# TensorE's wait for the low halves of the weights: one wait for two units in place of one for each

## The chip, the cores and the metric

The kernel runs on one core of one Trainium2 chip. The metric is the device time of one execution in microseconds (us), lower is better. A run's time is the median of several executions of the same program on the chip, and a profile is the record that the hardware profiler made of one execution.

## The reference

The input is a sequence of 256 tokens of width 2048 in float32. Two transformer blocks follow each other.

```
# block 1
h = x + fox_mixer(rms_norm(x))          # 16 heads of 128, causal softmax with a forget gate
h = h + conv_ffn(rms_norm(h))           # up to 2 x 5632, 3-tap convolution, silu(gate) * val, down
# block 2
a = rms_norm(h); qa, ka, va, ra, ga, qb, kb, vb = split(a @ w_in)
log_g = log_sigmoid(ga @ gate_w2 + gate_b) / 16
out_a = gla_mixer(qa, ka, va, ra, log_g)        # 4 heads, chunks of 64, gated linear attention
out_b = dilated_mixer(rms(qb), rms(kb), vb, rel_bias)   # 8 heads, three dilation patterns
h = h + concat(out_a, out_b) @ w_out
h = h + (silu(n @ w_gate) * (n @ w_up)) @ w_down, with n = rms_norm(h)
```

The time goes to the products with the weights: in all 788 x 0.5 MiB of float32 weights pass through the core once.

## The kernel before, in words

The weights are stored as one stream of 788 units. A unit is a tile of 128 partitions x 1024 float32 values, that is eight blocks of 128 x 128. Activations lie transposed (features on partitions, 256 tokens along the free axis), and each product is made from split numbers: a weight is written as a high half `whi` and a low half `wlo`, both in the format float32r, and the activations likewise as `x[:, kc, 0, :]` and `x[:, kc, 1, :]`. For each block TensorE multiplies `whi` with both halves of the activations (512 columns) and `wlo` with the high half (256 columns). VectorE later folds the two 256-column halves of the PSUM bank into one (L943).

Four slots (RING = 4) hold units in flight, each with `raw`, `whi` and `wlo`. Unit u lies in slot u mod 4. A unit passes through these steps:

- SyncE loads it into `raw[slot]` (L278), once the low half of the unit four before it is made.
- ScalarE copies `raw` to `whi` (split_hi, L654). It waits for the load, and for `unit_used`, which says that TensorE is done with the unit four before it.
- VectorE makes `wlo = raw - whi` (split_lo, L937) and raises `lo_ready` by one.
- TensorE waits for `lo_ready` and runs the 16 matmuls of the unit (L345 and L346). The last one raises `unit_used`.

The order of each engine's work is written out by hand. With AHEAD = 3, step k of ScalarE's and VectorE's programs splits unit k + 3, among the other work of that step: VectorE takes finished chunks out of PSUM (take, L943 and L977, which raises `chunk_out`), does the softmax, the gates and the residual sums, and ScalarE does squares, exponentials, logarithms and copies. TensorE's own order is units in sequence, with small matmuls between them.

The stages in order are: one unit pair for the forget gates (units 0 and 1), the heads of layer 1 with six units each (from unit 2), its output projection, up projection (from unit 130) and down projection (from unit 306), then the same for layer 2 (from unit 394): one unit pair for the gate ranks, four gated heads of 12 units from unit 396, eight heads of six units, output, up and down projection. Most stages are hardware loops in which the unit's number is a register's value. Every loop advances by a multiple of four units, so a unit's slot is known when the program is built and an even slot is an even unit.

At the start, VectorE does in this order: low halves of x chunks 0 to 3, split of unit 0, x chunks 4 to 11, split of unit 1, x chunks 12 to 15, splits of units 2 and 3, eight sums of squares (L970), split of unit 4, eight more sums, split of unit 5, split of unit 6, the forget gates' take and first steps (L943 to L1187), the first head's query take, split of unit 7. ScalarE makes the high halves in the same order, with the squares between the splits of 3 and 4 and of 4 and 5. Behind the high half of unit 5 it waits for the mean of squares, which TensorE makes behind unit 4 (norm_mean, L366), for rstd by a Ln (L667) and an Exp (L669), and only then makes the high halves of 6 and 7. TensorE's unit 6 waits for the forget gates' take as well (`chunk_out`). Behind unit 7 stands the first head's mean (head_mean, L371), which waits for ScalarE's squares of query and key (L674).

In the first gated head TensorE makes the gates' matmuls (L598) behind unit 398. VectorE and ScalarE turn them into decays (L1304 to L1317, L904 to L911) ahead of the splits of units 402 and 403. Behind unit 403 stand the matmuls of L428, which wait for `g_kd` (L1096).

Of the kernel before, what the change touches and what calls it, by code (L numbers as in the profile page):

```python
# [96 lines left out]
def build(nc, wstream, xt, vectors, identity, dist_onehot, rel_bias, gate_w2, scan_keep, gla_mask, fox_mask, out):  # L97
    with ExitStack() as ctx:
# [3 lines left out]
        def sem(name):  # L102
            return ctx.enter_context(nc.semaphore(name))
# [108 lines left out]
        hi_ready, lo_ready, unit_used = sem("hi_ready"), sem("lo_ready"), sem("unit_used")  # L212
# [122 lines left out]
        def _(pe):  # L335
            def unit(pos, k, blocks, x):

                slot = pos.slot(k)
                pe.wait_ge(lo_ready, pos.unit(k) + 1)
                for j, (bank_no, kc, first, last, late) in enumerate(blocks):  # L340
                    if late:
                        pe.wait_ge(*late)
                    w_hi = whi[slot][:, j * P:(j + 1) * P]
                    w_lo = wlo[slot][:, j * P:(j + 1) * P]
                    pe.matmul(acc[bank_no][:, :], w_hi, x[:, kc, :, :].rearrange("p a s -> p (a s)"), start=first, stop=False)  # L345
                    mm = pe.matmul(acc[bank_no][:, S:2 * S], w_lo, x[:, kc, 0, :], start=False, stop=last)  # L346
                mm.then_inc(unit_used, 1)

            def half(pos, k, bank_no, part, x, late=None):

                late = late or {}
                unit(pos, k, [(bank_no, 8 * part + j, part == 0 and j == 0, part == 1 and j == 7, late.get(8 * part + j))
                              for j in range(BLOCKS)], x)
# [180 lines left out]
            def down(layer):  # L534

                with pe.Fori(0, 2) as i:
                    pos = Pos(layer.unit_down, U_DOWN // 2, i)

                    pe.wait_ge(hid_split, FC * (layer.n + 1) - 1)
                    for k in range(U_DOWN // 2):  # L540
                        blocks = []
                        for b in range(BLOCKS * k, BLOCKS * (k + 1)):
                            c, kc = divmod(b, FC)
                            if kc == 0:
                                pe.wait_ge(chunk_out, layer.chunk_down + 8 * i + c - 3)

                            late = (hid_split, FC * (layer.n + 1)) if b == FC - 1 else None
                            blocks.append((c % 4, kc, kc == 0, kc == FC - 1, late))
                        unit(pos, k, blocks, hid2)
# [52 lines left out]
            for c in range(6):  # L602
                pe.wait_ge(chunk_out, L1.chunk_heads + c - 2)
                for part in range(2):
                    k = 2 * c + part
# [12 lines left out]
            for j in range(2):  # L618
                chunk = DIL.chunk0 + 3 * j
                n = DIL.count0 + j  # L620
                for c in range(3):
                    pe.wait_ge(chunk_out, chunk + c - 2)
                    for part in range(2):
                        k = 2 * c + part
# [823 lines left out]
```

## Time and profile before

| | us |
|---|---|
| median of 3 runs (2330.54 to 2330.74) | 2330.71 |
| the profiled execution | 2330.62 |
| its span, first to last instruction | 2328.8 |
| TensorE matmuls busy | 2306.4 (99%) |
| VectorE busy | 1611.0 (69%) |
| ScalarE busy | 1220.8 (52%) |

Busy times count instructions that work on data. TensorE's matmuls and weight loads are shown as two engines, PE and PEld, since they overlap; both are issued by one sequencer. DVE is VectorE, ACT is ScalarE, SP is SyncE. Starts are counted from the beginning of the span. "L345" is line 345 of the kernel.

### The profile page before, as it was taken

Reading aid. Unit: us, or ns where it says so; the run is one execution under the profiler, and the core shown is the slowest. Engines: PE = TensorE matmul, PEld = TensorE weight load, DVE = VectorE, ACT = ScalarE, POOL = GpSimd, SP = SyncE. Lnnn points to the kernel's source line nnn. Section 1 sums busy time; section 2 is a strip of 40 time slices with the busy share of each in tenths; the row PEclk is TensorE's granted clock in tenths of the full one; section 3 lists DMA queues with packets and bytes.
Section 4 is the critical chain, followed back from the end, with each engine's and each line's share of the span. In section 5 each row is a group of like instructions: output and inputs, shape, how many; then the busy total and the mean of one; then the engine's idle time right before and its main releaser. Section 6 shows DMA issues by size and latency. Waiting matters only on the chain.

```text
span 2328.8 us, 39072 instructions
## 1 busy us (share of the span) xinstructions
PE 2306.4 (99%) x13218; PEld 1998.6 (86%) x13218; DVE 1611.0 (69%) x2339; ACT 1220.8 (52%) x1574; POOL 22.3 (1%) x45
## 2 busy tenths in 40 slices
PE   7999999999999999999999999999999999999999
PEld 5888888888888888888878888888888888888888
DVE  7767677788888888555566667677666667664554
ACT  6666665655555555444455466655444444443332
POOL 0000000000000000000000000000000000000000
PEclk9999999999999999999999999999999999999999
DMA  6555545555555555655555444455555555555553
GB/s 213 166 168 179 176 161 182 186 191 189 186 191 191 189 186 184 198 189 186 188 165 165 166 159 160 158 184 189 189 189 189 189 189 190 189 188 192 198 193 131
DMA packets 118513, 423.39 MB, mean 182 GB/s; under 512 B 13629, under 2 KB 15829, under 8 KB 118464
## 3 DMA queue, kind: packets, MB, share of 16 engines
q1 hardware_dynamic: 114048, 415.29, 53.6%
q0 software_dynamic: 1968, 5.13, 0.8%
q10 hardware_dynamic: 2448, 2.32, 0.3%
q8 instruction: 31, 0.51, 0.1%
q14 instruction: 18, 0.15, 0.0%
HBM read 420.55 MB, written 3.70 MB: 182 GB/s over the span
## 4 chain that ended last, share of the span: by engine, by line
PE 97%; DVE 1%; ACT 0%; issue 0%; DMA 0%; SPq 0%; DVEq 0%; ACTq 0%
PE acc L345 62%; PE acc L346 31%; PE b_mean L371 1%; PE b_score L382 0%; DMA xres<-xt 0%; DVE wlo L937 0%; PE b_turn L390 0%; PE b_mean L463 0%; PE b_mean L464 0%; PE b_score L381 0%; PE b_mean L396 0%; PE b_val L377 0%; PE b_mean L397 0%; PE b_mean L398 0%; DVE sq_sum L970 0%
## 5 line engine op out<-in xcount | busy, mean ns | idle before, releaser
L345 PE MATMUL acc<-xs,whi 128*128 128x512 f32 x4384 | 1549.2, 398 | 15.3 <-DVE wlo L937 12.9
L654 ACT ACTIVATE whi<-raw 128x1024 fp32r<-128x1024 f32 x788 | 831.5, 1059 | 871.6 <-PE acc L346 862.4
L937 DVE TENSOR_TENSOR wlo<-raw,whi 128x1024 fp32r<-128x1024 f32 x788 | 961.4, 1223 | 407.2 <-ACT whi L654 403.9
L346 PE MATMUL acc<-xs,wlo 128*128 128x256 f32 x4384 | 1225.8, 280 | 0.0
L345 PEld LDWEIGHTS acc<-xs,whi 128*128 128x128 f32 x4384 | 823.1, 188 | 213.4 <-DVE wlo L937 14.9
L346 PEld LDWEIGHTS acc<-xs,wlo 128*128 128x128 f32 x4384 | 828.3, 189 | 5.5 <-issue 5.3
L345 PE MATMUL acc<-hid,whi 128*128 128x512 f32 x1408 | 494.5, 395 | 0.0
L346 PE MATMUL acc<-hid,wlo 128*128 128x256 f32 x1408 | 396.4, 282 | 0.0
L943 DVE TENSOR_REDUCE folded_t<-acc 128x256 f32<-128x512 f32 (+1 forms) x338 | 233.3, 690 | 158.4 <-PE acc L346 146.9
L345 PEld LDWEIGHTS acc<-hid,whi 128*128 128x128 f32 x1408 | 264.8, 188 | 62.2
L346 PEld LDWEIGHTS acc<-hid,wlo 128*128 128x128 f32 x1408 | 264.4, 188 | 0.0
L345 PE MATMUL acc<-mix,whi 128*128 128x512 f32 x512 | 182.6, 398 | 0.0
L346 PE MATMUL acc<-mix,wlo 128*128 128x256 f32 x512 | 144.5, 282 | 0.0
L345 PEld LDWEIGHTS acc<-mix,whi 128*128 128x128 f32 x512 | 96.2, 188 | 23.5 <-issue 0.5
L346 PEld LDWEIGHTS acc<-mix,wlo 128*128 128x128 f32 x512 | 96.3, 188 | 0.5 <-issue 0.5
L769 ACT ACTIVATE hid<-hid 128x256 f32 (+1 forms) x88 | 36.0, 409 | 52.4 <-DVE hid L1140 52.2
L984 DVE SCALAR_TENSOR_TENSOR qk_n<-qk,qk_gain,rstd_qk 128x256 f32<-128x256 f32 x48 | 21.1, 482 | 53.1 <-ACT rstd_qk L680 53.1
L977 DVE TENSOR_TENSOR up_v<-folded_t,rstd 128x256 f32<-128x256 f32 x88 | 37.5, 427 | 3.0
L977 DVE TENSOR_TENSOR up_g<-folded_t,rstd 128x256 f32<-128x256 f32 x88 | 37.5, 426 | 3.0
L1144 DVE TENSOR_TENSOR hid<-hid,hid 128x256 f32 (+1 forms) x88 | 36.9, 419 | 1.0 <-ACT hid L769 1.0
L754 ACT ACTIVATE tap_g<-up_g,vec 128x256 f32<-128x256 f32 x44 | 26.5, 602 | 16.3 <-DVE up_g L977 16.3
L762 ACT ACTIVATE tap_v<-up_v,vec 128x256 f32<-128x256 f32 x44 | 26.5, 603 | 15.3 <-DVE up_v L977 15.2
(169 smaller groups left out, 924.9 us busy)
## 6 DMA issues: line engine op xcount, KB each, us to landing
raw<-wstream SPq DMA_DIRECT2D x788, 512.0 KB, 3.4
xres<-xt SPq DMA_DIRECT2D x4, 512.0 KB, 8.3
decay_row<-decay_scratch POOLq DMA_DIRECT2D x16, 128.0 KB, 3.5
out<-xres ACTq DMA_DIRECT2D x16, 128.0 KB, 2.3
dist_scratch<-bias_scratch POOLq DMA_DIRECT2D x8, 192.0 KB, 3.7
toeplitz<-dist_scratch POOLq DMA_DIRECT2D x8, 128.0 KB, 3.8
vec<-vectors ACTq DMA_DIRECT2D x1, 213.5 KB, 5.2
g_keep<-scan_keep POOLq DMA_DIRECT2D x1, 128.0 KB, 3.1
```

The lines of the kernel that those rows point to most:

```text
L345: pe.matmul(acc[bank_no][:, :], w_hi, x[:, kc, :, :].rearrange("p a s -> p (a s)"), start=first, stop=False)
L346: mm = pe.matmul(acc[bank_no][:, S:2 * S], w_lo, x[:, kc, 0, :], start=False, stop=last)
L371: pe.matmul(b_mean[:, :], mean_h[:, :], sq_qk[:, :, :].rearrange("p a s -> p (a s)"), start=True, stop=True).then_inc(qk_mean, 1)
L654: act.activation(whi[slot][:, :], raw[slot][:, :], ACT.Copy).then_inc(hi_ready, 1)
L754: act.activation(tap_g[:, :], up_g[:, 0:S], ACT.Identity, scale=column("conv0", j), bias=column("convb", j)).then_inc(tap0, 1)
L762: act.activation(tap_v[:, :], up_v[:, 0:S], ACT.Identity, scale=column("conv0", FC + j), bias=column("convb", FC + j)).then_inc(tap0, 1)
L769: act.activation(hid2[:, j, 0, :], hid[:, :], ACT.Copy).then_inc(hid_hi_ready, 1)
L937: dve.tensor_tensor(wlo[slot][:, :], raw[slot][:, :], whi[slot][:, :], ALU.subtract).then_inc(lo_ready, 1)
L943: dve.tensor_reduce(folded_t[0:rows, :], acc[bank_no][0:rows, :].rearrange("p (a s) -> p s a", a=2), AX_X, ALU.add).then_inc(chunk_folded, 1)
L977: dve.tensor_tensor(dst, folded_t[0:rows, :], rstd[0:rows, :], ALU.mult).then_inc(chunk_out, 1)
L984: dve.scalar_tensor_tensor(out=qk_n[:, a, :], in0=qk[:, a, :], scalar=qk_gain[:, col + a:col + a + 1], in1=rstd_qk[:, a, :], op0=ALU.mult, ...
L1144: dve.tensor_tensor(hid2[:, j, 1, :], hid[:, :], hid2[:, j, 0, :], ALU.subtract).then_inc(hid_split, 1)
```

## The change

Only units in even slots wait for `lo_ready`, and they wait for one unit more: their own low half and that of the unit behind them. Units in odd slots have no wait of their own.

```diff
             def unit(pos, k, blocks, x):
 
                 slot = pos.slot(k)
-                pe.wait_ge(lo_ready, pos.unit(k) + 1)
+                if slot % 2 == 0:
+                    pe.wait_ge(lo_ready, pos.unit(k) + 2)
                 for j, (bank_no, kc, first, last, late) in enumerate(blocks):
```

## Rows read from the trace of the kernel before

**Rows 1.** The page, part 1: busy us (share of the span) xinstructions.

```profile
PE 2306.4 (99%) x13218; PEld 1998.6 (86%) x13218; DVE 1611.0 (69%) x2339; ACT 1220.8 (52%) x1574; POOL 22.3 (1%) x45
```

**Rows 2.** View of waits, PEld: engine, line, released by: us in total, times, longest.

```profile
PEld acc L345 <- DVE wlo L937: 14.9, 6, 11.0
```

**Rows 3.** Page, part 5: count | busy, mean ns | idle before.

```profile
L937 DVE TENSOR_TENSOR wlo<-raw,whi 128x1024 fp32r<-128x1024 f32 x788 | 961.4, 1223 | 407.2 <-ACT whi L654 403.9
```

**Rows 4.** Timeline of PEld, 11 to 45 us: start, us, what [idle before <-releaser].

```profile
11.04 0.29 PEld L345 LDWEIGHTS acc<-xs,whi 128*128 128x128 f32 x1 [11.04 <-DVE wlo L937]
...
15.88 0.19 PEld L345 LDWEIGHTS acc<-xs,whi 128*128 128x128 f32 x1 [0.29 <-DVE wlo L937]
...
18.69 0.19 PEld L345 LDWEIGHTS acc<-xs,whi 128*128 128x128 f32 x1
...
25.24 0.19 PEld L345 LDWEIGHTS acc<-xs,whi 128*128 128x128 f32 x1 [0.95 <-DVE wlo L937]
...
29.29 0.30 PEld L366 LDWEIGHTS b_mean<-sq_sum,mean_d 128*128 128x128 f32 x2 [1.32 <-DVE sq_sum L970]
...
30.88 0.19 PEld L345 LDWEIGHTS acc<-xs,whi 128*128 128x128 f32 x1 [0.87 <-DVE wlo L937]
...
36.38 0.19 PEld L345 LDWEIGHTS acc<-xs,whi 128*128 128x128 f32 x1 [2.73 <-DVE f L977]
...
39.60 0.19 PEld L345 LDWEIGHTS acc<-xs,whi 128*128 128x128 f32 x1 [0.49 <-DVE wlo L937]
...
44.06 0.30 PEld L371 LDWEIGHTS b_mean<-sq_qk,mean_h 128*128 128x128 f32 x2 [1.69 <-issue]
```

**Rows 5.** View of line 339 (the wait): register operations, ns min/median/max, starts.

```profile
L339 PEldq ALU_OP  x651: 32/32/42, 63.4 to 2319.3; - x163
```

**Rows 6.** Timeline at unit 308, of PEld and of DVE.

```profile
928.32 0.19 PEld L345 LDWEIGHTS acc<-hid,whi 128*128 128x128 f32 x1
...
927.32 3.69 DVE L937 TENSOR_TENSOR wlo<-raw,whi 128x1024 fp32r<-128x1024 f32 x3
```

**Rows 7.** Timeline of DVE at the start: the splits of units 1, 5 and 7.

```profile
14.60 1.23 DVE L937 TENSOR_TENSOR wlo<-raw,whi 128x1024 fp32r<-128x1024 f32 x1 [0.44 <-ACT whi L654]
...
29.60 1.23 DVE L937 TENSOR_TENSOR wlo<-raw,whi 128x1024 fp32r<-128x1024 f32 x1 [0.37 <-ACT whi L654]
...
38.33 1.22 DVE L937 TENSOR_TENSOR wlo<-raw,whi 128x1024 fp32r<-128x1024 f32 x1
```

**Rows 8.** Timeline of ACT at the start: table load, Ln, square of the key.

```profile
29.59 1.28 ACT L667 ACT_TABLE_LOAD   x1
30.88 0.47 ACT L667 ACTIVATE ln_x<-b_mean,eps 128x256 f32<-128x256 f32 x1
...
43.53 0.42 ACT L674 ACTIVATE sq_qk<-qk 128x256 f32<-128x256 f32 x1 [1.79 <-DVE qk L977]
```

**Rows 9.** Timeline at units 402 and 403, of PEld and of DVE.

```profile
1193.35 0.19 PEld L345 LDWEIGHTS acc<-xs,whi 128*128 128x128 f32 x1
...
1197.35 0.19 PEld L345 LDWEIGHTS acc<-xs,whi 128*128 128x128 f32 x1 [1.22 <-DVE wlo L937]
...
1201.82 0.31 PEld L428 LDWEIGHTS b_score<-g_qt,g_kt 128*64 128x64 f32 x8 [1.69 <-DVE g_kd L1096]
...
1196.08 2.35 DVE L937 TENSOR_TENSOR wlo<-raw,whi 128x1024 fp32r<-128x1024 f32 x2
```

**Rows 10.** Timeline at unit 424, of PEld and of DVE (split of 425).

```profile
1270.94 0.19 PEld L345 LDWEIGHTS acc<-xs,whi 128*128 128x128 f32 x1
...
1269.24 1.22 DVE L937 TENSOR_TENSOR wlo<-raw,whi 128x1024 fp32r<-128x1024 f32 x1
```

**Rows 11.** Timeline of PE; and the windows view (PEclk is the granted clock).

```profile
11.84 0.63 PE L345 MATMUL acc<-xs,whi 128*128 128x512 f32 x1
...
2325.18 0.28 PE L346 MATMUL acc<-hid,wlo 128*128 128x256 f32 x1
...
2329.30:2330.00 0.70, 0.00 (x0) 0.00 (x0) 0.00 (x0) 0.00 (x0) 0.00 (x0) 0.50 0.00 0
```

## Prediction

> **What bounds the kernel now.** I read the page's busy shares first: TensorE works 99% of the span [rows 1]. So any idle time added to TensorE comes out at the end one for one, unless it fills idle time that is there already. Next comes the view of waits, taken on TensorE's weight loads because the wait that is changed stands ahead of them: waits for VectorE's `wlo` (the low halves) sum to only 14.9 us in 6 places, 11.0 of it ahead of the first unit [rows 2]. Then the group of L937: the split itself takes 1.22 us a unit [rows 3]. A unit of TensorE takes 2.81 us (15.88 to 18.69 [rows 4]), so a split normally has room. What matters is how early the low half of unit u+1 lies before unit u starts. I numbered the units by their first weight load and matched them with the 788 splits, in order. The program's own order fixes this lead: at step k ScalarE and VectorE split unit k+3, after unit k-1 has freed its slot. So while unit u runs, the split of u+3 is made, and at the start of u those of u+1 and u+2 are normally there.
>
> **What the change removes.** Odd units (every second one, 394 of 788) lose their wait. TensorE's sequencer shows 651 register operations of 32 ns at that line over the run, as far as the waits stand in loops [rows 5]. They run beside matmuls: the loads of unit 1 to unit 2 and unit 308's show no extra pitch [rows 4, 6]. I book 0. The bounds: nothing, and a gain of half of them, 325 x 0.032 = 10.4 us, if each were exposed. The first is far nearer to the rows, since a whole 8-block unit at 2.81 us holds no stall at its edge.
>
> **What it adds.** An even unit u now waits for the split of u+1 too. No split is made later for that reason alone, until TensorE itself is late. Behind TensorE's wait stand all its later matmuls, and behind those `unit_used` (ScalarE's next splits, VectorE's takes) and the next weight load. The wait bites in three places.
>
> (1) The start, units 0 to 8. Unit 1's split ends at 14.60 + 1.23 = 15.83 [rows 7]; unit 0 starts there, at 15.88, and no longer at 11.04. Units 0 to 3 then run back to back: 4.55 us for the first (11.04 to 15.88 less 0.29 idle [rows 4], it is slow) and 3 x 2.81, to 28.9. Unit 2 needs the splits of 2 and 3. These use their slots for the first time, so nothing of TensorE holds them, and before the two units ran without a pause (18.69 to 25.24 less 0.95 idle is 2 x 2.8 [rows 4]): the split of 3 is made by 21.5, and unit 2 now starts at 23.2, no wait. Unit 4 (25.24 before) must wait for the split of unit 5, 29.60 + 1.23 = 30.83 [rows 7]. That one does not move: ScalarE's share of it stands behind its squares, and unit 1, whose slot it needs, is done at 23.2. So all that was lost in units 0 to 3 is hidden behind this later wait. Unit 4 starts at 30.88 and ends at 33.7.
> Behind unit 4 stands the sum-of-squares matmul (norm_mean), 29.29 before [rows 4], at 33.7 now. Its result was early before: ScalarE's Ln waited for its table until 29.59 + 1.28 = 30.87 and started at 30.88 [rows 8]. Now the mean lands at 33.7 + 0.7 = 34.4, Ln starts near 34.5: 3.6 us late. From there to the split of unit 7 VectorE and ScalarE hold no slack (Ln, table, Exp, split 6, forget-gate take, query take, split 7), so it ends at 38.33 + 1.22 + 3.6 = 43.15 [rows 7]. TensorE meanwhile does norm_mean and the distance bias (their weight loads ended 0.87 us ahead of 30.88, at 30.0; with the bias matmuls some 1.2 us from 29.29, an estimate) and unit 5, 35.0 to 37.8. Unit 6 before waited only for the forget-gate take, to 36.38, and unit 7 for its own split, to 39.60 [rows 4]. Now unit 6 waits for the split of unit 7 and starts at 43.2; unit 7 follows without a pause and ends at 43.2 + 2 x 2.82 = 48.85. The head's mean matmul (L371), which waited for ScalarE's square until 44.06 before [rows 4, 8], finds it done (43.95 + 3.6 = 47.6) and goes at 48.85. So the start costs 48.85 - 44.06 = 4.8 us. Unit 8 then asks for the split of 9, made near 48.2: no wait.
>
> (2) Unit 308, third of the first down projection. The convolution's last work holds up VectorE; three splits run together from 927.32 for 3.69 us, the first of which is unit 309's, done at 928.54, against a start of unit 308 at 928.32 [rows 6]. Cost 0.27 us.
>
> (3) Unit 402, where layer 2's gates are made. The gate chain holds the split of unit 403 to 1196.08 + 1.22 = 1197.30. Before, unit 402 ran from 1193.35 under it, and TensorE waited 1.22 us ahead of 403 and 1.69 ahead of the L428 matmuls for `g_kd` [rows 9]. Now unit 402 starts at 1197.36, 403 at 1200.18, and L428 at 1203.0 in place of 1201.82: `g_kd` depends on neither unit, so of the 4.0 us of stall 2.8 fill idle time that was there. Cost 1.2 us.
>
> Elsewhere the u+1 split is early enough. The smallest margin in the repeated stages is that of the second gated head: unit 425's split ends at 1269.24 + 1.22 = 1270.46, unit 424 starts at 1270.94 [rows 10], 0.48 us left (three such heads); the same subtraction for the even units of the other repeated stages gives 1.1 us or more. These margins move with TensorE, so the delays above do not eat them.
>
> Sum: 4.8 + 0.27 + 1.2 = 6.2 us, no gain against it.
>
> (4) The clock. The first matmul of unit 0 shown takes 0.63 us [rows 11], and the unit 4.55 in place of 2.81: 1.2 GHz at first, 2.4 GHz soon after. TensorE's longest idle before was 2.73 us on the weight loads (36.38 [rows 4]), and unit 6 behind it ran at full pace. After the last matmul, which ended at 2325.18 + 0.28 = 2325.46 [rows 11], the granted clock was down to 0.50 by 2329.30, 3.8 us later. The new stall ahead of unit 6 is 37.8 to 43.2, over 5 us. So here I expect the clock to fall, and units 6 and 7 to pay for it in full, as nothing behind them waits for anyone else. Price: that of the cold first unit, 4.55 - 2.81 = 1.7 us; bounds 0 (it holds) and twice that, 3.5 (it comes back late). The stall ahead of 402, 3.8 us, stands on the edge; I leave it warm in the sum.
> The Trainium skill (TensorE: Matmul & The Clock Gate, section "Why this matters for your kernels") says the same of idle gaps between bursts: one long enough throws the clock back to half, and it calls the moment variable from run to run. By that rule both stalls may pay; by the 2.73 us row alone neither would. No run yet decides for gaps between.
>
> Total: 6.2 + 1.7 = 7.9 us. The profiled execution took 2330.62 (span 2328.8 and 1.8 around it), the median is 2330.71; 2330.7 + 7.9 = 2338.6.
>
> **Rivals.**
> A. The clock holds over both stalls: 2330.7 + 6.2 = 2336.9. For it: no gap before ever cost pace. Against: 0.50 at 3.8 us after the last matmul.
> B. The clock falls at both stalls, or comes back late: 6.2 + 2 x 1.7 = 9.6, so 2340.3; with the late return at the first, 2342.
> C. The start's loss is mostly hidden: units 6 and 7 overlap a wait that I took as moving (say the Ln chain shortens because its table is already loaded, or the take of unit 7 has slack). Then 2 to 4 us are left in all: 2333 to 2335, within 0.2%. Against it: the split of unit 7 at 38.33 has no idle time ahead of it [rows 7], so VectorE came to it straight from its chain.
> D. The other side: dropped waits give pace. If TensorE's sequencer, not its array, sets the time at odd units, each of the register operations saved is worth its 32 ns: 10.4 us off, 6.2 on, 2326.5 with a warm clock. It decides in favour from 19 ns saved per odd unit (7.9/394 = 0.020 us). Against: no idle mark stands at unit 2's start, whose wait had long been met [rows 4].
> E. The new condition bites in every repeated head, as semaphores arrive later than the profile's ends: 0.48 us of margin would have to be lost, three times; under 1 us, inside the range.
>
> **How the numbers follow.** Forecast (falls once) 0.44, A 0.30, B 0.13, C 0.08, D 0.05. A change under 0.2% (4.7 us, 2326.0 to 2335.4) can't be told from none. The range takes in the forecast with its own bounds, A less 1.1 us for the estimates in its chain (the 3.6, the 1.2), and B's lower price with 0.9 above it: 2335.8 to 2341.2. Slower by over 0.2% has the forecast, A and B, 0.87; within holds C and part of D, 0.10; faster 0.03.
>
> **What would show it.** Right: the first weight load of unit 0 at 15.9, unit 4's at 30.9, unit 6's near 43.2 with over 5 us idle ahead put down to `wlo` L937; L371 near 50.5 (48.9 if the clock held); hi matmuls of unit 6 at 0.63; a stall near 4 us ahead of unit 402 while that ahead of L428 is gone; unit 308 with 0.27. The waits for `wlo` grow from 14.9 us to about 31 (15.9 + 2.0 + 5.3 + 0.3 + 4.0 and some), yet the end moves by under 10, as part of that fills old waits. Wrong: stalls on `wlo` in the repeated stages; L371 before 47 us; pace changes in the steady stages; a total under 2335.4.

## The result, and the profile after

| | before | after |
|---|---|---|
| median, us | 2330.58 (2330.47 to 2330.74, 5 runs) | 2341.80 (2340.47 to 2344.92, 5 runs) |
| ratio | 1 | 1.0053 (95%: 1.0041 to 1.0064) |
| profiled execution, us (its span) | 2330.62 (2328.8) | 2341.80 (2340.0) |
| TensorE matmuls busy, us | 2306.4 | 2311.1 |

The change costs 11.2 us, where 7.9 was forecast. All line numbers of the changed kernel are one higher from line 340 on (TensorE's high matmul is L346 there, the split L938, L371 is L372).

The weight loads of the changed kernel at the start. They answer to [rows 4].

```profile
15.80 0.29 PEld L346 LDWEIGHTS acc<-xs,whi 128*128 128x128 f32 x1 [15.80 <-DVE wlo L938]
...
20.88 0.33 PEld L346 LDWEIGHTS acc<-xs,whi 128*128 128x128 f32 x1
...
24.17 0.19 PEld L346 LDWEIGHTS acc<-xs,whi 128*128 128x128 f32 x1
...
30.82 0.19 PEld L346 LDWEIGHTS acc<-xs,whi 128*128 128x128 f32 x1 [1.15 <-DVE wlo L938]
...
33.64 0.30 PEld L367 LDWEIGHTS b_mean<-sq_sum,mean_d 128*128 128x128 f32 x2
...
35.01 0.19 PEld L346 LDWEIGHTS acc<-xs,whi 128*128 128x128 f32 x1 [0.64 <-issue]
...
43.16 0.29 PEld L346 LDWEIGHTS acc<-xs,whi 128*128 128x128 f32 x1 [5.38 <-issue]
...
48.24 0.33 PEld L346 LDWEIGHTS acc<-xs,whi 128*128 128x128 f32 x1
...
51.50 0.30 PEld L372 LDWEIGHTS b_mean<-sq_qk,mean_h 128*128 128x128 f32 x2
...
52.04 0.19 PEld L346 LDWEIGHTS acc<-xs,whi 128*128 128x128 f32 x1 [0.24 <-issue]
```

The starts on which the chain rests are where it put them: unit 0 at 15.80, unit 4 at 30.82, the mean of squares at 33.64, unit 5 at 35.01, unit 6 at 43.16. Between them unit 2 came at 24.17 and not at 23.2: units 0 and 1 together took 8.4 us (15.80 to 24.17), where the chain had 7.4. Unit 4's wait shrank by it (1.15 us idle), so it cost nothing. From unit 6 on the two part. Units 6 and 7 take 8.3 us to L372 (43.16 to 51.50) and not 5.7. The 5.38 us stall of the weight loads carries the mark "issue", but the view of the matmuls names the split for it, and for the stall ahead of unit 402:

```profile
43.19 0.77 PE L346 MATMUL acc<-xs,whi 128*128 128x512 f32 x1 [5.09 <-DVE wlo L938]
...
1207.97 0.77 PE L346 MATMUL acc<-xs,whi 128*128 128x512 f32 x1 [3.81 <-DVE wlo L938]
```

The next two fences show ScalarE and VectorE on the chain that made the split of unit 7 late, and answer to [rows 8] and [rows 7].

```profile
29.52 1.28 ACT L668 ACT_TABLE_LOAD   x1
34.38 0.47 ACT L668 ACTIVATE ln_x<-b_mean,eps 128x256 f32<-128x256 f32 x1 [3.57 <-PE b_mean L367]
```

```profile
41.83 1.22 DVE L938 TENSOR_TENSOR wlo<-raw,whi 128x1024 fp32r<-128x1024 f32 x1
```

The Ln starts 3.5 us later than before, now on TensorE's mean. The split of unit 7 ends at 43.05, and unit 6 starts 0.1 us after it.

One matmul of unit 6, and the windows view over both places (busy time of each engine, then the granted clock, DMA share and GB/s):

```profile
43.97 0.63 PE L346 MATMUL acc<-xs,whi 128*128 128x512 f32 x1
```

```profile
39.00:42.00 3.00, 0.00 (x0) 0.00 (x0) 2.86 (x8) 1.10 (x2) 0.00 (x0) 1.00 0.53 175
42.50:49.20 6.70, 6.01 (x19) 5.18 (x20) 5.56 (x10) 3.58 (x7) 1.06 (x2) 0.50 0.51 169
49.30:52.00 2.70, 2.70 (x15) 2.20 (x15) 1.41 (x2) 0.51 (x1) 0.17 (x1) 1.00 0.76 206
1202.00:1206.00 4.00, 2.16 (x13) 1.60 (x11) 3.96 (x6) 3.42 (x4) 0.00 (x0) 1.00 0.25 101
1206.50:1213.20 6.70, 5.23 (x16) 4.49 (x17) 5.71 (x9) 2.13 (x3) 0.00 (x0) 0.50 0.58 168
```

The clock fell to 0.50 (1.2 GHz) while TensorE still stood, at either stall, and stayed there for most of two units each time. (The view prints 1.00 ahead of the trace's first record of the clock too, so the slow start has to be read from the weight loads: 0.33 us at 20.88, 0.19 at 24.17.) Around unit 402 the weight loads, which answer to [rows 9]:

```profile
1207.94 0.29 PEld L346 LDWEIGHTS acc<-xs,whi 128*128 128x128 f32 x1 [4.11 <-issue]
1213.02 0.29 PEld L346 LDWEIGHTS acc<-xs,whi 128*128 128x128 f32 x1
...
1216.14 0.31 PEld L429 LDWEIGHTS b_score<-g_qt,g_kt 128*64 128x64 f32 x8 [0.25 <-issue]
```

The 1.69 us wait for `g_kd` is gone, as forecast, but unit 402 takes 5.08 us and 403 3.1.

At unit 308, TensorE's weight loads for the high halves and VectorE's splits, which answer to [rows 6]:

```profile
935.90 0.19 PEld L346 LDWEIGHTS acc<-hid,whi 128*128 128x128 f32 x1 [0.32 <-DVE wlo L938]
...
938.00 0.19 PEld L346 LDWEIGHTS acc<-hid,whi 128*128 128x128 f32 x1
938.37 0.19 PEld L346 LDWEIGHTS acc<-hid,whi 128*128 128x128 f32 x1
938.71 0.19 PEld L346 LDWEIGHTS acc<-hid,whi 128*128 128x128 f32 x1
```

```profile
934.63 3.69 DVE L938 TENSOR_TENSOR wlo<-raw,whi 128x1024 fp32r<-128x1024 f32 x3
```

The stall is the forecast 0.27 us (a pitch of 0.62 in place of 0.35). But behind it the pitch of a block is no longer 349 ns throughout: it runs 349, 351, 360 in turn, 353.3 in the mean, for the 86 units that are left of the stage. Counting TensorE's matmuls in 30 us (first and second down projection), before:

```profile
1000.00:1030.00 30.00, 30.00 (x174) 26.28 (x174) 16.74 (x19) 13.08 (x15) 0.00 (x0) 1.00 0.58 188
2200.00:2230.00 30.00, 30.00 (x172) 26.16 (x171) 15.17 (x15) 11.16 (x11) 0.00 (x0) 1.00 0.56 191
```

and after:

```profile
1000.00:1030.00 30.00, 30.00 (x173) 26.13 (x172) 16.72 (x19) 12.71 (x15) 0.00 (x0) 1.00 0.55 186
2200.00:2230.00 30.00, 30.00 (x174) 26.27 (x173) 15.42 (x15) 11.64 (x11) 0.00 (x0) 1.00 0.63 199
```

The counts alone are coarse; the starts of units 310 to 393 and 704 to 787 give 348.9 and 353.3 ns a block before, 353.3 and 348.9 after, at full clock in each.

Comparing the starts of the same unit in the two profiles gives the whole account: +7.45 us at unit 8, settling at +7.31 by unit 20; +0.27 at unit 308; +3.05 over the rest of the first down projection; +3.69 at unit 404; -3.09 over the second down projection. Sum 11.2, the difference of the spans.

### The profile page after: what moved, and what is told of

The parts are those of the page before. It is cut to its first block, busy times and chain, and to the rows that moved or that the text cites. A ratio compares the mean times of both kernels' runs of the same rounds, so it can differ in the third digit from the quotient of the medians.

```text
span 2340.0 us, 38704 instructions
## 1 busy us (share of the span) xinstructions
PE 2311.1 (99%) x13218; PEld 1998.6 (85%) x13218; DVE 1610.9 (69%) x2339; ACT 1220.8 (52%) x1574; POOL 22.3 (1%) x45
## 4 chain that ended last, share of the span: by engine, by line
PE 98%; DVE 1%; DMA 0%; ACT 0%; issue 0%; SPq 0%; DVEq 0%; ACTq 0%
PE acc L346 62%; PE acc L347 31%; PE b_mean L372 1%; PE b_score L383 0%; DMA xres<-xt 0%; PE b_turn L391 0%; DVE wlo L938 0%; PE b_mean L464 0%; PE b_mean L465 0%; PE b_score L382 0%; PE b_mean L397 0%; PE b_val L378 0%; PE b_mean L399 0%; PE b_mean L398 0%; DVE sq_sum L971 0%
## 5 line engine op out<-in xcount | busy, mean ns | idle before, releaser
L346 PE MATMUL acc<-xs,whi 128*128 128x512 f32 x4384 | 1554.2, 400 | 25.5 <-DVE wlo L938 25.5
L938 DVE TENSOR_TENSOR wlo<-raw,whi 128x1024 fp32r<-128x1024 f32 x788 | 961.2, 1223 | 414.5 <-ACT whi L655 411.3
L346 PEld LDWEIGHTS acc<-xs,whi 128*128 128x128 f32 x4384 | 826.4, 189 | 228.2 <-issue 18.6
L346 PE MATMUL acc<-hid,whi 128*128 128x512 f32 x1408 | 494.5, 395 | 0.0
L346 PEld LDWEIGHTS acc<-hid,whi 128*128 128x128 f32 x1408 | 264.7, 188 | 62.8 <-DVE wlo L938 0.3
L346 PE MATMUL acc<-mix,whi 128*128 128x512 f32 x512 | 182.6, 398 | 0.0
L346 PEld LDWEIGHTS acc<-mix,whi 128*128 128x128 f32 x512 | 96.2, 188 | 23.7 <-issue 0.5
```

Source lines behind the costliest of these rows:

```text
L938: dve.tensor_tensor(wlo[slot][:, :], raw[slot][:, :], whi[slot][:, :], ALU.subtract).then_inc(lo_ready, 1)
```

## The experiments

Theory after the result: the waits cost what was forecast (6.3), half clock behind both long stalls costs some 2.5 each, and the paces of the down projections cancel in this pair of profiles. Rivals: a loss spread over the steady stages; late splits and not the clock behind the stalls; a pace drawn by chance and untouched by the change.

**Undoing the places one by one.** In the changed kernel, the units of the named places wait for themselves again:

```diff
-                if slot % 2 == 0:
+                u = pos.base + k
+                if not pos.per and (u < 8):        # e1;  e2: 402 <= u < 404;  e3: both
+                    pe.wait_ge(lo_ready, u + 1)
+                elif slot % 2 == 0:
                     pe.wait_ge(lo_ready, pos.unit(k) + 2)
```

`pos.base` is the number of a stage's first unit, and `pos.per` is 0 outside loops. e4 is e3 with `pos.base == 306 and k in (2, 3)` added: units 308 and 309, and 352 and 353, which have their places in the loop's second pass.

> Units 0 to 7 wait as in the kernel before; all other units wait in pairs. Theory (stalls plus clock): the start costs the change 4.8 us of waiting and 2.5 us of half clock (unit 8 starts 7.4 us later in the profile after), so this comes back 7.3 us below the changed kernel, near 2334.5, with unit 8 at 44.6 and no clock fall before unit 402; the stall and the fall at 402 stay. Rival (the loss is spread over the steady stages, as the waits or the pace of the matmuls got worse everywhere): under 3 us come back.

> Only units 402 and 403 wait as before; all others wait in pairs. Theory: 1.2 us of waiting and 2.5 us of half clock come back at 402, so 3.7 us below the changed kernel, near 2338.1; the low clock is granted once, behind the start. Rival: the clock falls there because of the long gate stage itself, not because of the stall: then only 1.2 us come back and the profile shows a low clock there still.

> Units 0 to 7 and 402 and 403 wait as before, all others in pairs. Theory: only the 0.27 us stall ahead of unit 308 is left, no clock fall: 2331.0, but the pace of the two down projections may differ from before by 3.1 to 3.3 us each (353 ns a block in place of 349, or the other way round), as it did in the profile after. If the stall at 308 sets the slow pace of the first down projection, that stage is slow here and fast in the fourth kernel. Rival: odd waits dropped make the steady stages faster or slower by a part of a nanosecond a block, seen in the starts of units 130 to 306.

> Units 0 to 7, 402 and 403 wait as before, and so do the units in the places of 308 and 309 in the down projections' loop of layer 1; all others in pairs. Theory: no stall is left: 2330.7 if the pace of the down projections is that of the kernel before. If the stall at 308 is what turned the first down projection from 349 to 353 ns a block, it is at 349 here. If it is not the stall but where the stage's instructions lie, or chance, it need not be.

| kernel | median, us | range | runs | ratio to before (95%) |
|---|---|---|---|---|
| e1, start undone | 2334.99 | 2333.50 to 2338.06 | 10 | 1.0025 (1.0016 to 1.0035) |
| e2, 402 undone | 2338.25 | 2337.00 to 2338.50 | 6 | 1.0038 (1.0026 to 1.0051) |
| e3, both undone | 2330.83 | 2330.53 to 2333.90 | 10 | 1.0004 (0.9994 to 1.0014) |
| e4, and 308 | 2330.68 | 2327.48 to 2333.83 | 10 | 0.9999 (0.9988 to 1.0010) |
| before, beside them | 2330.50 | 2327.39 to 2334.10 | 27 | |

Against the changed kernel's 2341.8, 6.8 and 3.6 us come back, where 7.3 and 3.7 were expected, and nothing measurable is left when both places are undone. The medians mix the levels told of below, so the starts of units are the firmer ground: e1 starts unit 8 at 44.89, 7.15 us sooner than the changed kernel, and e2 takes 3.80 us less than it from unit 394 to unit 404 (33.91 and 37.71). Units 140 to 300 take 443.73 us (346.7 ns a block) in every profile of this document, with the odd waits or without them, so some 390 dropped waits are worth nothing either way: the spread loss and the gain from fewer waits both fall. In e2 the clock stayed at 1.00 through the gate stage; its stalls there are those of before (1.22 and 1.69 us), so the long gate stage alone does not bring the clock down.

In e1's profile one thing was not expected, though the start is that of the kernel before:

```profile
36.53 0.24 PEld L350 LDWEIGHTS acc<-xs,whi 128*128 128x128 f32 x1 [2.73 <-DVE f L982]
...
40.86 0.19 PEld L350 LDWEIGHTS acc<-xs,whi 128*128 128x128 f32 x1
...
44.89 0.19 PEld L350 LDWEIGHTS acc<-xs,whi 128*128 128x128 f32 x1 [0.39 <-issue]
```

```profile
36.70:40.00 3.30, 3.30 (x11) 2.82 (x12) 3.23 (x9) 2.44 (x5) 0.00 (x0) 0.50 0.48 159
```

Here the same 2.73 us wait as in [rows 4] did bring the clock down, and unit 6 took 4.33 us. Unit 8 still started only 0.3 us later than before: the wait for the split and for the square behind it swallowed the loss. So my argument from that row, that a gap of 2.73 us costs no pace, rested on one execution.

**The three levels.** The executions of the kernel before, which lay within 0.3 us at first, fell into three groups in the later comparisons: near 2327.5, 2330.6 and 2333.8. They are 3.1 us apart, as a down projection at 353.3 and one at 348.9 are (704 blocks x 4.4 ns), and the profiles agree: both stages are fast in e6's of 2327.54, one is slow in e3's and e4's of 2330.7 and 2330.8, both are in e5's of 2333.96. In the four sets of runs beside the experiments their numbers were 13/8/6, 7/17/3, 15/11/3 and 3/2/4. e3, which keeps the stall at 308, had none of 10 in the lowest group; e4, without it, had 4 of 10. Hence the next two, each one edit of the kernel before, which asks for more at one even unit and drops no wait:

```diff
-                pe.wait_ge(lo_ready, pos.unit(k) + 1)
+                pe.wait_ge(lo_ready, pos.unit(k) + (2 if pos.base == 306 and k == 2 else 1))   # e6: k == 6
```

> The kernel before with one edit: in the loop of the first down projection the third unit (308 in the first pass) waits for the split of 309 too. Theory (a stall at 308 locks the stage into the slow pace): down projection 1 at 353.3 ns a block in the profile, no timed run near 2327.5, most at 2330.8 and some at 2333.9. Rival (chance alone sets the pace of both stages, as the kernel before has runs at 2327.5, 2330.6 and 2333.8): the same three levels in about the same shares as the kernel before.

> The kernel before with the same edit at the seventh unit of that loop (312), where the split of the next one is over 2 us early: the same instructions less, no stall. If the stall is what pins the pace, this one has the three levels of the kernel before, with runs near 2327.5. If what matters is that TensorE's instruction stream is shorter there, it behaves as the one with the stall: none near 2327.5.

e5: 2333.82 (11 runs; 1 in the lowest group, 3 in the middle, 7 in the highest), ratio 1.0010 (1.0001 to 1.0019). e6: 2330.73 (11 runs; 4, 2 and 5), ratio 1.0005 (0.9996 to 1.0014). The weight loads of e5 at the stall:

```profile
928.07 0.19 PEld L345 LDWEIGHTS acc<-hid,whi 128*128 128x128 f32 x1
...
928.69 0.19 PEld L345 LDWEIGHTS acc<-hid,whi 128*128 128x128 f32 x1 [0.32 <-DVE wlo L937]
```

The block starts of the profiles tell more than the times. In each up projection they come in one of two rhythms of the same mean, 346.7 ns: 348, 345, 348, 345, or 347, 346, 347. The first enters the down projection at 348.9, the second at 353.3. That held at all 20 entries of the ten profiles that have no extra matmul right ahead of a down projection (before, after, e1 to e7 and the repeat e12). In six of them (after, e1, e2, e3, e5, e12) the first down projection entered at the fast pace and went over to 351, 360, 349 within three blocks of the stall at 308; in before, e4 and e6, without that stall, it stayed fast. e5 drops no wait and slows down, e4 drops nearly all odd ones and does not. So the stall, not the dropped waits, moves the stage; but one run of 11 of e5 in the lowest group says that it does not do so every time. The rhythm is much older than the down projection: in all 28 up projections of the profiles the one that ends the stage stands from its third unit on, and its first two units already differ. What draws it ahead of them is open.

**The clock.** The changed kernel, with matmuls that nobody reads put ahead of the two waits:

```diff
+                fill = {6: (20, b_turn), 402: (14, b_val)}.get(pos.base + k) if not pos.per else None
+                for _ in range(fill[0] if fill else 0):
+                    pe.matmul(fill[1][:, :], xs[:, 0, 0, 0:P], xs[:, 0, :, :].rearrange("p a s -> p (a s)"), start=True, stop=True)
                 if slot % 2 == 0:
```

> The changed kernel, with matmuls that nobody reads put ahead of the waits of units 6 and 402 (20 and 14 of 512 columns, some 4.6 and 3.2 us, less than either stall). Theory (the two long stalls cost half clock as well): no low clock in the profile before the end, units 6 and 7 in 2.8 us each, 2.5 us less at each place: 5.0 below the changed kernel, 2336.8 with the pace as there. Rival (the price behind the stalls is not the clock but the late splits of the next units): nothing comes back, 2341.8.

The windows view of it at the two places, and the weight loads of units 6, 8, 402 and 404 (L349 here):

```profile
39.00:44.00 5.00, 4.18 (x18) 3.49 (x19) 4.86 (x12) 3.14 (x5) 0.00 (x0) 1.00 0.33 107
44.30:50.10 5.80, 5.80 (x34) 5.01 (x33) 4.97 (x6) 2.36 (x3) 1.06 (x2) 1.00 0.70 203
1206.70:1212.40 5.70, 5.70 (x32) 4.82 (x32) 5.41 (x8) 1.76 (x2) 0.00 (x0) 1.00 0.73 245
```

```profile
44.25 0.19 PEld L349 LDWEIGHTS acc<-xs,whi 128*128 128x128 f32 x1
...
50.54 0.19 PEld L349 LDWEIGHTS acc<-xs,whi 128*128 128x128 f32 x1 [0.24 <-issue]
...
1206.63 0.19 PEld L349 LDWEIGHTS acc<-xs,whi 128*128 128x128 f32 x1 [0.96 <-DVE wlo L941]
...
1213.03 0.19 PEld L349 LDWEIGHTS acc<-xs,whi 128*128 128x128 f32 x1
```

The clock held at both. Unit 402 to 404 took 6.39 us, not 8.75: 2.4 back. (The wait alone thus cost 3.69 - 2.36 = 1.3 there.) At the start the filling began only behind the older wait for `chunk_out`, at 39.8, and ran past the split, so unit 6 came at 44.25, 1.1 us later than in the changed kernel; even so unit 8 started at 50.54, 1.5 us before the changed kernel's 52.04. From unit 6 to unit 8 it took 6.30 us and not 8.88: the half clock's price is 2.6. The split of unit 7 was on time at 41.77 + 1.22, so late splits are not the price; the clock is. The whole ran at 2340.59 (2339.81 to 2341.54, 4 runs), 1.2 below the changed kernel and not the expected 5.0: in the profile 3.7 us came back by unit 494, and then the second down projection ran at 353.3 and took 3.1 of it.

**Trying to set the rhythm.** The kernel before with matmuls on `b_val` ahead of each down projection: one of 128 x 128 (e8), two of them (e9), one of 512 columns (e10), one of 256 (e11).

```diff
             def down(layer):
 
+                for _ in range(2):                # e9;  e8: once
+                    pe.matmul(b_val[:, 0:P], xs[:, 0, 0, 0:P], xs[:, 0, 0, 0:P], start=True, stop=True)
```

> The kernel before with one matmul of 128 x 128 ahead of each down projection, read by nobody: it moves the stage's start by about 0.1 to 0.4 us and its instructions by a few places, with no wait. If the pace is set by how the stage is entered, the shares of the three levels change from those of the kernel before; if each stage draws its pace by chance whatever comes ahead, they stay. A cost of its own of under 1 us in either case.

> The kernel before with two matmuls of 128 x 128 ahead of each down projection, read by nobody. With one such, both stages ran at 353.3 ns a block in all executions. Theory (TensorE's stream of weight loads and matmuls has two stable rhythms, and anything that breaks the alternation at the entry can push it from one to the other): a fixed level again, and with two it may be the fast one, near 2327.7 (two of 348.9). Rival (any extra work at the entry makes the stage slow): 2334.1, as with one.

> The kernel before with one matmul of 512 columns ahead of each down projection, read by nobody: the form of a high matmul, 0.23 us each, 0.5 in all. Theory: the rhythm of each stage is set anew; both fast would be 2327.9, both slow 2334.3. Rival (any extra work makes the stage slow): 2334.3. If the entry does not matter, three levels as in the kernel before.

> The same with one matmul of 256 columns, the form of a low matmul, 0.12 us each. Theory: a fixed level or other shares than before; both fast 2327.7, both slow 2334.0. Rival as in the two before.

| kernel | median, us | lowest / middle / highest group | ratio (95%) |
|---|---|---|---|
| e8 | 2333.95 | 0 / 0 / 11 | 1.0016 (1.0007 to 1.0025) |
| e9 | 2333.93 | 0 / 4 / 7 | 1.0016 (1.0007 to 1.0024) |
| e10 | 2334.20 | 0 / 0 / 11 | 1.0019 (1.0011 to 1.0028) |
| e11 | 2330.90 | 1 / 7 / 4 | 1.0009 (1.0001 to 1.0018) |

A single small matmul decides over 3 us a stage: all 22 executions of e8 and e10 lie in the highest group, and in their two profiles both stages run at 353.3. In the profiles of e9 and e11 a stage entered in the 347 rhythm came out fast and one in the 348, 345 rhythm slow: the extra work turned them round. "Any extra work makes it slow" falls with these two, "chance alone" with e8 and e10. None pins the fast pace, so no version beats the kernel before.

**The changed kernel again.**

> The changed kernel itself, unedited, to see the spread of its executions. Theory (stall at the start 4.8, at 402 1.2, half clock behind each of the two, stall at 308 0.3 which also pushes the first down projection from 348.9 to 353.3 ns a block, 3.1): its fastest execution lies near 2327.5 + 6.3 + 5.0 + 3.1 = 2341.9 less what a shorter low clock saves, none within 10 us of the lowest level of the kernel before, 2327.5; a second group about 3.1 higher, where the second down projection is slow too. The profile shows a unit-long pitch of 0.35 to 0.6 us at the entry of unit 308 and 353.3 behind it. Rival (the first down projection draws its pace by chance in the changed kernel as well): some executions near 2338.8.

2341.14 (2340.25 to 2343.52, 5 runs), ratio 1.0042 (1.0028 to 1.0057), beside a kernel before at 2330.60 (9 runs). With the first five runs these are ten, six from 2340.25 to 2341.80 and four from 2343.50 to 2344.92, none near the 2338.8 of a pace drawn afresh. Its profile (2343.52), in the windows view and in the weight loads of units 6, 8, 402 and 404:

```profile
40.50:47.20 6.70, 3.83 (x12) 3.28 (x13) 6.60 (x14) 4.31 (x6) 0.49 (x1) 0.50 0.44 153
1207.90:1211.20 3.30, 3.30 (x12) 2.82 (x11) 3.27 (x6) 0.12 (x1) 0.00 (x0) 0.50 0.82 211
```

```profile
43.34 0.29 PEld L346 LDWEIGHTS acc<-xs,whi 128*128 128x128 f32 x1 [5.43 <-issue]
...
51.22 0.19 PEld L346 LDWEIGHTS acc<-xs,whi 128*128 128x128 f32 x1 [0.24 <-issue]
...
1207.32 0.19 PEld L346 LDWEIGHTS acc<-xs,whi 128*128 128x128 f32 x1 [4.11 <-issue]
...
1215.25 0.19 PEld L346 LDWEIGHTS acc<-xs,whi 128*128 128x128 f32 x1
```

The clock was low at both places, but for less of TensorE's work. At the start it fell while 2.9 us of the stall were left, and units 6 and 7 took 7.88 us, 1.6 and not 2.6 more than the 6.30 of e7. At 402 it fell 0.5 us after the unit had started (403 started 4.34 us after 402, and 404 3.58 after that), which cost 1.5 and not 2.4 us. Set beside the time that TensorE worked at 0.50, the price is even: 6.1 and 5.3 us of such work cost 2.6 and 2.4 us in the first profile, 3.9 and 3.4 us cost 1.6 and 1.5 in this one, 0.40 to 0.45 us for each. These prices, with the level, make up the spread that the changed kernel has.

## Why the prediction was wrong

- **No gain from dropped waits** (booked 0): right. The pace of the up projection did not change in any profile, and the two paces of the down projections are those of the kernel before. (Rival D's break-even is 20 ns by its own division, not 19.)
- **The start, 4.8 us of waiting**: right, and so is the chain, but for the first units, which lost 2.7 us to the low clock in place of 1.7 and hid it behind unit 4's wait. 51.50 - 44.06 = 7.44, less 2.6 of half clock, is 4.8; e1's profile gave 7.15 of both back.
- **Unit 308, 0.27 us**: right in the stall, wrong in what follows it. The stall also costs 3.1 us wherever the stage had entered at the fast pace. In the two profiles it doesn't show in the end, by luck: the kernel before ran its second down projection slow and the changed kernel its first, 3.05 and -3.09. Against the lowest group of the kernel before it counts in full.
- **Unit 402, 1.2 us**: right (1.3). The `g_kd` wait took up the rest.
- **The clock, step (4)**: the step that failed. "The stall ahead of 402, 3.8 us, stands on the edge; I leave it warm in the sum": it fell there in each of after, e1 and e12, which cost 2.4, 1.4 and 1.5 us (402 to 404 less 6.39). And the price of one fall was taken from the cold first unit, 1.7 us, of a stream that started 4.0 us before the clock rose (11.04, and 15.03 in the trace). Behind the stalls of the profile after it was 2.6 and 2.4, as TensorE worked at the low clock for 6.1 and 5.3 us. So the clock cost 5.0 us where 1.7 were in the sum, and that is the whole of the miss. Rival B, with two falls, had the right mechanism at 2340.3; with the measured prices it is 2330.6 + 6.3 + 5.0 = 2341.9. I gave it 0.13, because I let one trace say that a gap of 2.73 us is harmless and 3.8 us the edge. The 2.73 us gap of the kernel before, 2.41 between the matmuls, did it in e1, e4, e6 and e9 to e11 (in some of them just after unit 6 had started), and not in before, e3, e5 and e8.
- The rule of the Trainium skill that I weighed against this (TensorE: Matmul & The Clock Gate, "Why this matters for your kernels") was the better guide: both stalls paid. That the moment varies from run to run stands in the same page's section "What you observe", of the clock's rise; here the fall moved as well, and the same place cost 2.4 us in one execution and 1.5 in another.
- **The sum of waits** was to grow to 31 us, though the terms named for it add up to 27.5. The view of TensorE's matmuls shows 25.5 in 4 waits. On the weight loads the five stalls add up to 26.8 (15.8, 1.15, 5.38, 0.32 and 4.11), and that view files two long ones, 5.38 and 4.11, under "issue".

## What to carry to other kernels

A wait that asks for more than it needs costs nothing where the producer runs ahead, so look only at the few places where it does not (starts, changes of stage), and walk those chains instruction by instruction. Add to each new stall of several microseconds on TensorE the half clock behind it, and take its price from the time that the engine then works at the low clock (here 0.40 to 0.45 us for each), not from one cold start. Before comparing a kernel at the level of 0.1%, see whether its times come in groups: here one stage's pace alone moved them by 3.1 us, and five runs that happened to agree hid it.

## What the runs showed that I had not expected

The same stream of weight loads and matmuls, with no wait in it and the clock at 1.00, has two steady paces in the down projections, 348.9 and 353.3 ns a block. A 0.27 us stall, or one extra matmul, can move it from one to the other for the rest of the stage. A low clock behind a gap of 2.7 us can be free, where a later wait absorbs it (unit 6 1.5 us longer in e1, unit 8 0.3 later).
